# Sliding-window attention in a two-layer decoder trunk: probabilities times values with the values as stationary operand, in split single-pass form

## What is computed

```python
def swa_sink_attention(q, k, v, sinks):
    # 16 query heads on 2 key/value heads of 64; blocks of 128 queries; keys: 16 meta, previous block, own block
    k_all, v_all = band(k), band(v)
    s = jnp.einsum('bnqkgd,bnskd->bnkgqs', qb, k_all) * (DH_B ** -0.5)
    s = jnp.where(allowed[None, :, None, None], s, NEG_INF)
    mx = jnp.maximum(jnp.max(s, axis=-1, keepdims=True), sink)
    pr = jnp.exp(s - mx)
    denom = jnp.sum(pr, axis=-1, keepdims=True) + jnp.exp(sink - mx)
    w = pr / denom
    o = jnp.einsum('bnkgqs,bnskd->bnqkgd', w, v_all)

# a layer, as a whole
mixed = concat([ya * silu(ga), yb * silu(gb), yc * silu(gc)])   # HGRN2 recurrence, attention, pooling
return h + mixed @ w_out
```

## Time and profile before

| what | value |
|---|---|
| median of three runs | 1631.59 us |
| the profiled execution's own time | 1631.37 us |
| its span in the profile | 1629.6 us |
| PE / PEld busy | 99% / 91% |
| DVE / ACT / POOL busy | 56% / 40% / 1% |
| TensorE clock granted | full (2.4 GHz) |
| share of PE in the chain that ended last | 96% |

### The profile page before, as it was taken

The page is one execution under the profiler, slowest core; times in us unless marked ns, Lnnn a source line. Parts: engine busy times, 40 slices in busy tenths (PEclk is TensorE's granted clock), DMA queues, the critical chain, the costliest instruction groups (busy, mean ns, idle before and its releaser), DMA issues.

```text
span 1629.6 us, 27470 instructions
## 1 busy us (share of the span) xinstructions
PE 1609.7 (99%) x11174; PEld 1481.2 (91%) x11174; DVE 915.1 (56%) x1897; ACT 645.5 (40%) x1280; POOL 20.8 (1%) x78
## 2 busy tenths in 40 slices
PE   6999999999999999999999999999999999999999
PEld 6999999999999999999998899888999878888887
DVE  7777877645666554434335678774555664443231
ACT  7676455423223332323237774553223233232121
POOL 0000000000000000000000000000000000000000
PEclk9999999999999999999999999999999999999999
DMA  6222211112121222434342221111212212234441
GB/s 252 84 100 78 79 34 46 53 53 78 53 78 53 80 102 85 150 118 157 118 144 79 103 78 53 53 52 53 78 53 78 72 59 101 81 130 138 135 156 65
DMA packets 28013, 147.22 MB, mean 90 GB/s; under 512 B 3568, under 2 KB 3696, under 8 KB 12656
## 3 DMA queue, kind: packets, MB, share of 16 engines
q1 hardware_dynamic: 27888, 145.46, 25.5%
HBM read 136.86 MB, written 8.52 MB: 89 GB/s over the span
## 4 chain that ended last, share of the span: by engine, by line
PE 96%; DVE 2%; issue 1%; ACT 0%; DMA 0%; SPq 0%; DVEq 0%
PE ps_gemm L798 80%; PE ps_mix L688 3%; PE ps_mix L724 3%; PE ps_mix L640 2%; PE ps_mix L654 2%; PE ps_mix L683 1%; PE ps_gemm L616 1%; DVE rstd L883 1%; PE ps_mix L768 1%; PE ps_mix L770 0%; PE ps_mix L700 0%; PE ps_mix L757 0%; PE ps_mix L719 0%; DVE w_lo L865 0%; DMA w_stage<-in_w_in 0%
## 5 line engine op out<-in xcount | busy, mean ns | idle before, releaser
L798 PE MATMUL ps_gemm<-x_hi,w_hi 128*128 128x264 f32 (+1 forms) x2240 | 560.7, 315 | 12.4 <-DVE w_lo L865 10.2
L798 PE MATMUL ps_gemm<-x_hi,w_lo 128*128 128x264 f32 (+1 forms) x2240 | 542.3, 307 | 0.0
L798 PE MATMUL ps_gemm<-x_lo,w_hi 128*128 128x264 f32 (+1 forms) x2240 | 541.8, 307 | 0.0
L798 PEld LDWEIGHTS ps_gemm<-x_hi,w_hi 128*128 128x128 f32 x2240 | 363.5, 189 | 34.9 <-DVE w_lo L865 11.0
L798 PEld LDWEIGHTS ps_gemm<-x_hi,w_lo 128*128 128x128 f32 x2240 | 363.1, 189 | 19.3
L798 PEld LDWEIGHTS ps_gemm<-x_lo,w_hi 128*128 128x128 f32 x2240 | 362.5, 189 | 16.4
L865 DVE TENSOR_TENSOR w_lo<-w_stage,w_hi 128x512 fp32r<-128x512 f32 x464 | 305.5, 689 | 104.0 <-ACT w_hi L422 92.6
L422 ACT ACTIVATE w_hi<-w_stage 128x512 fp32r<-128x512 f32 x464 | 265.4, 618 | 169.5 <-DVE z L943 122.7
L798 PE MATMUL ps_gemm<-mixed_hi,w_lo 128*128 128x264 f32 (+1 forms) x768 | 205.3, 322 | 0.0
L798 PE MATMUL ps_gemm<-mixed_lo,w_hi 128*128 128x264 f32 (+1 forms) x768 | 205.0, 321 | 0.0
L798 PE MATMUL ps_gemm<-mixed_hi,w_hi 128*128 128x264 f32 (+1 forms) x768 | 203.8, 320 | 0.0
(11 more groups left out here) (169 smaller groups left out, 1407.4 us busy)
## 6 DMA issues: line engine op xcount, KB each, us to landing
w_stage<-in_w_in SPq DMA_DIRECT2D x83, 1024.0 KB, 4.8
w_stage<-in_w_out SPq DMA_DIRECT2D x32, 1024.0 KB, 5.2
x_in<-in_xT SPq DMA_DIRECT2D x4, 1056.0 KB, 9.9
res<-in_xT SPq DMA_DIRECT2D x16, 264.0 KB, 5.4
h1T<-z SPq DMA_DIRECT2D x16, 264.0 KB, 5.8
res<-h1T SPq DMA_DIRECT2D x16, 264.0 KB, 5.2
out<-z SPq DMA_DIRECT2D x16, 256.0 KB, 5.5
rope<-in_c_rope SPq DMA_DIRECT2D x2, 528.0 KB, 4.7
```

The lines of the kernel that those rows point to most:

```text
L798: ins = pe.matmul(g[:, bank, 0:size], ws, xs[:, k, c:c + size], start=tick == 0 and i == 0, stop=tick == TICKS - 1 and i == 2)
```

## The change

- **Values as weights.** `values` now makes the output with head dimensions as rows and the queries of two heads as 256 moving columns. The values `a_v` are split in high and low halves side by side in the 128 weight columns; the transposed probabilities are split too (`a_pt_hi` by ScalarE, `a_pt_lo` by VectorE, `att_probs_low`). All are float32r. Rows of the other 64 hold the product with the low half of the values; ScalarE copies them out (`a_out_lo`), VectorE adds (`att_out`), for each batch, straight into `y`. `outputs_t` and `att_normalise` go.
- **Meta keys.** GpSimd splits the meta columns in two instructions; VectorE spreads the transposed ones into a block-diagonal operand of 512 columns (L1171 of the new kernel), and one float32r matmul of 128 rows takes them with `a_vmeta`. Its values are loaded by eight small transfers instead of four.
- **Reciprocals at the end.** The sums of all batches are collected in `a_den`; after the last batch VectorE inverts them, TensorE transposes them, SyncE writes them to memory and loads them spread over 64 rows (slots 22 and 24; 16 transfers for each half in layer 0, 8 in layer 1); VectorE multiplies four tiles of `y` in slot 23 and four in slot 25, tick 6.
- **The table.** Jobs are now spaced by the batch: 1.0 tick for b = 0, 1.6 for b = 1, 1.9 for the others.
- **Order on VectorE.** In a tick the low halves and the sums stand ahead of the meta spread and the masked maximum.
- **GpSimd takes `w_lo`** for the chunks 12 to 20 of a layer, which is made in slots 11 to 19.
- In slot 2 ScalarE copies the values in four pieces and VectorE takes four differences.

```diff
-    if at < 0 or (at and at * 5 // 8 == (at - 1) * 5 // 8):
+CELL_TICKS = {0: 1.0, 1: 1.6, 2: 1.9, 3: 1.9, 4: 1.9}
+LEAD_TICKS, TAIL_TICKS, TAIL_CELLS = 1.0, 1.2, 18
+RECIP_LOAD_SLOTS, RECIP_SLOTS, RECIP_TICK = (22, 24), (23, 25), 6
+WLO_POOL = range(ATT_SLOT + 1, 21)
...
# SyncE
+                if n == RECIP_LOAD_SLOTS[0]:
+                    rows = 4 * len(ATT_B[layer])
+                    sp.wait_ge(s_rde, layer + 1)
+                    sp.dma_start(rdD[0:rows], rdt[0:rows]).then_inc(s_rdo, 16)
+                    sp.wait_ge(s_rdo, 16 * (layer + 1))
+                    load_recips(layer, 1)
+                if n == RECIP_LOAD_SLOTS[1]:
+                    sp.wait_ge(s_rdm, 8 * layer + 4)
+                    load_recips(layer, 0)
...
# GpSimd
+            def w_low(N, q):
+                pool.wait_ge(s_whi, 4 * N + q + 1)
+                pool.tensor_tensor(wl[:, N % 3, ks], wst[:, N % 3, ks], wh[:, N % 2, ks].bitcast(F32), ALU.subtract)
+            def probs_meta(layer, q, pair):
+                pool.tensor_copy(pmc[0:nq, Q % 2, 0, heads], src).then_inc(s_apc, 1)
+                pool.wait_ge(s_apc, 2 * Q + pair + 1)
+                pool.tensor_tensor(pmc[0:nq, Q % 2, 1, heads], src, pmc[0:nq, Q % 2, 0, heads].bitcast(F32),
+                                   ALU.subtract).then_inc(s_apm, 1)
...
# ScalarE, lag OUT_LAG = 13
+                        act.wait_ge(s_apv, 2 * Q + 2)
+                        act.activation(ol[rows, 0:4 * nq], M[other, 3, 0:4 * nq], ACT.Copy).then_inc(s_aol, 1)
...
# TensorE
+            def values(layer, q, pair):
+                if pair == 0 and Q:
+                    pe.wait_ge(s_aod, Q)
                 if b:
-                    for i in range(4):
-                        for s in range(0 if b >= 2 else 1, 2):
-                            last = pe.matmul(o[:, DH * i:DH * i + DH], pts[:, i // 2, i % 2, s],
-                                             vb[:, b - 1 + s, DH * kv:DH * kv + DH],
-                                             start=False, stop=i == 3 and s == 1)
+                    pe.wait_ge(s_apl, pairs_before(layer, q) + pair + 1)
+                    for s in range(first, 2):
+                        for part in (pth, ptl):
+                            ins = pe.matmul(M[:, 3, 256 * pair:256 * pair + 256], vs[:, b - 1 + s, kv],
+                                            part[:, s, heads].rearrange("p i q -> p (i q)"),
+                                            start=pair == 0 and s == first and part is pth, stop=False)
+                if pair == 1:
+                    pe.wait_ge(s_ame, Q + 1)
+                    pe.matmul(M[:, 3, 0:4 * nq], vm[:, kv], bd[:, :, 0:nq], start=b == 0, stop=True)\
+                      .then_inc(s_apv, 1 if b else 2)
-                pe.transpose(M[0:64, 1, BAND:BAND + nq], pmc[0:nq, Q % 2].rearrange("p i k -> p (i k)"), eye[0:nq, 0:nq])\
+                pe.transpose(M[:, 1, BAND:BAND + nq], both, eye[0:nq, 0:nq]).then_inc(s_amt, 1)
...
# VectorE
+            def att_probs_low(layer, q, pair):
+                dve.wait_ge(s_ape, no + 1)
+                signal(dve.tensor_tensor(ptl[:, first:2, heads],
+                                         M[:, 2].rearrange("p (s i q) -> p s i q", s=2, i=2)[:, first:2],
+                                         pth[:, first:2, heads].bitcast(F32), ALU.subtract), s_apl)
+            def att_apply_recips(layer, j):
+                dve.wait_ge(s_rdi, recip_loads(layer, 2 - j))
+                for i in range(4):
+                    m = 4 + 4 * j + i
+                    signal(dve.tensor_tensor(y[:, m, c], y[:, m, c], rdb[:, i, c], ALU.mult), s_rdm)
...
-                    if tick - 1 in HI_TICKS and N + 1 < NTOT:
+                    if tick - 1 in HI_TICKS and N + 1 < NTOT and not low_on_pool(N + 1):
                         w_low(N + 1, HI_TICKS.index(tick - 1))
```

More of the change, by code:

```diff
@@ L92, with recip_loads, att_cells, att_job @@
 ATT_Q0 = [0, len(ATT_B[0])]
+RECIP_LOAD_SLOTS, RECIP_SLOTS, RECIP_TICK = (22, 24), (23, 25), 6
+def recip_loads(layer, rounds):
+    return 16 * (16 * rounds if layer == 0 else 32 + 8 * rounds)
+def att_cells(layer):
+    jobs, t, at = ATT_B[layer], 0.0, {}
+    for c in range(ATT_LEAD + 4 * len(jobs) + TAIL_CELLS):
+        at[int(t)] = c
+        q = (c - ATT_LEAD) // 4
+        t += LEAD_TICKS if q < 0 else TAIL_TICKS if q >= len(jobs) else CELL_TICKS[jobs[q][0]]
+    return at
+ATT_CELL = [att_cells(l) for l in range(DEPTH)]
+def att_job(layer, n, tick):
+    at = (n - ATT_SLOT) * TICKS + tick - ATT_TICK
+    return ATT_CELL[layer][at] if at in ATT_CELL[layer] else None
+WLO_POOL = range(ATT_SLOT + 1, 21)
+def low_on_pool(N):
+    return N % NC in WLO_POOL
+def lows_before(N, pool):
+    return 4 * sum(low_on_pool(M) == pool for M in range(N))
 def pairs_before(layer, q):
@@ L297, in att_at @@
         def att_at(layer, n, tick, lag):
-            job = att_job(n, tick)
+            job = att_job(layer, n, tick)
             if job is None:
@@ L315, in att_pair_at @@
         def att_pair_at(layer, n, tick, job):
-            now = att_job(n, tick)
+            now = att_job(layer, n, tick)
             if now is None:
@@ L334, in load_w, with load_recips @@
                 sp.dma_start(wst[:, N % 3].rearrange("p k c -> p (k c)"), src).then_inc(s_w[N % 3], 16)
+            def load_recips(layer, j):
+                blocks = len(ATT_B[layer]) // 4
+                all_ = rdD[0:16 * blocks].rearrange("(b j v i) q -> j v i b q", j=2, v=2, i=4)
+                for kv in range(2):
+                    rows = slice(64 * kv, 64 * kv + 64)
+                    for i in range(4):
+                        real = all_[j, kv, i, blocks - NBLK:].unsqueeze(0).broadcast_to([64, NBLK, P])
+                        sp.dma_start(rdb[rows, i, N_META:].rearrange("p (b q) -> p b q", b=NBLK), real)\
+                          .then_inc(s_rdi, 16)
+                        if blocks > NBLK:
+                            meta = all_[j, kv, i, 0, 0:N_META].unsqueeze(0).broadcast_to([64, N_META])
+                            sp.dma_start(rdb[rows, i, 0:N_META], meta).then_inc(s_rdi, 16)
             def load_x(q):
@@ L820, in _ @@
                     at = att_at(layer, n, tick, VALUE_LAG)
-                    if at and at[1] == 0:
-                        values(layer, at[0])
+                    if at and at[1] < 2:
+                        values(layer, *at)
                     at = att_at(layer, n, tick, PAIR_LAG)
@@ L825, in _ @@
                         probs_t(layer, at[0], at[1] // 2)
[L826 to L828 removed]
+                    at = att_at(layer, n, tick, RECIP_T_LAG)
+                    if at and at == (len(ATT_B[layer]) - 1, 0):
+                        recips_t(layer)
                     h, r = hgrn_at(n, tick)
@@ L1249, in _ @@
                                                      ALU.subtract), s_ql)
+                    at = att_at(layer, n, tick, PAIR_LAG + 1)
+                    if at and at[1] % 2 == 1 and ATT_B[layer][at[0]][0]:
+                        att_probs_low(layer, at[0], at[1] // 2)
+                    at = att_at(layer, n, tick, OUT_LAG + 1)
+                    if at and at[1] == 0:
+                        att_out(layer, at[0])
                     at = att_at(layer, n, tick, META_LAG)
```

234 lines of the change are left out of this document (131 added, 103 removed).

## The result

The changed kernel takes **1642.88 us** (median of 4 runs, 1640.65 to 1646.06) against 1631.59 (1631.11 to 1631.74): ratio 1.0071, 95% interval 1.0056 to 1.0086. It is 0.7% slower; I had forecast 1602.4, and the result lies above the range. The profiled execution took 1643.33 us, its span is 1641.5.

The account below looks back on a forecast made before the run. TensorE's own work was taken to bound the kernel as long as VectorE keeps up. From 1631.4 us, -42.4 (TensorE), +9.4 (VectorE late in attention) and +4.0 (reciprocals) gave 1602.4 us, range 1589 to 1622.

Parts of the forecast that it names:

- TensorE, -42.4: TensorE's own work: cheaper values and meta keys, no transposes back, small additions; -42.4 us, between -45.4 and -39.6.
- rival 4: Value matmuls: the halves bring nothing if 256 columns take 0.31 us; +42 us, 1635 us in all; chance 0.04.
- The reciprocals, +4.0: Slot 25, tick 6: four VectorE multiplications delay TensorE's next level by 2.0 us in each layer, +4.0 us; slot 23 costs 0.
- GpSimd's hold, 1.5 us a slot: Attention slots: GpSimd subtractions keep VectorE's instructions with two SBUF inputs waiting, 1.5 us a slot (0 to 4).
- Rival 3: Slots 12 to 18 and 70 to 75: GpSimd subtractions stop VectorE for their whole 1.6 us; +81, 1674 us; chance 0.06.
- What reaches the end, +9.4: Attention: VectorE's time, with GpSimd's hold added, exceeds TensorE's in seven tight slots; +9.4 us, +0.5 without the hold.
- the seven slots to which I gave 9.4 us: Slots 12, 13, 14, 18, 71, 72 and 75, where VectorE was to exceed TensorE by 0.9 to 1.9 us each.
- The second: Attention: VectorE falls further behind, needing to be on time within a job; twice the 9.4, or late reciprocals; 1611 to 1622; 0.12.
- The first: Attention: VectorE keeps up and the hold costs nothing that reaches TensorE; 1593.5 us, or 1589; chance 0.25.

Follow-up runs that it names:

- e4: Changed kernel, nobody making the weights' low halves for chunks 12 to 20, and output copy and sum one job earlier: 1595.17 us, ratio 0.9778.
- e6: Changed kernel with output copy and sum one job earlier and the second four reciprocal multiplications in slot 26 instead of 25: 1608.4 us, ratio 0.9859.
- e1: Changed kernel with nobody making the weights' low halves for chunks 12 to 20 (third product takes the high half again): 1608.8 us, ratio 0.9862.
- e3: Changed kernel with ScalarE's output copy and VectorE's sum one job earlier (OUT_LAG 12 instead of 13): 1615.58 us, ratio 0.9904.
- e5: Changed kernel with all low halves of the weights back on VectorE and output copy and sum one job earlier: 1615.89 us, ratio 0.9908.

## Why the prediction was wrong

- **TensorE, -42.4: right, a little small.** Busy time fell by 45.4 us where little disturbs it (e4), and e4 still has one stretch of 3.4 us at half clock, so the work itself fell by up to 1.7 more. That is the outer end of my range; its own terms (0.115 a value matmul, entries and weights free) add up to -46.1, not the -45.4 I wrote. Value matmuls start 0.12 apart and the one for the meta keys takes 0.23; rival 4 fell.
- **The reciprocals, +4.0: right.** 3.8 by the lengths of slots 25 and 83 (e6), 3.8 of idle time in these slots in the change, where slot 83 has a stretch at half clock on top. The multiplications are 0.70 us each, and the 16 transfers were in time.
- **GpSimd's hold, 1.5 us a slot: right in size, in part by luck.** VectorE's busy time was lengthened by 28.8 us over 18 slots (957.5 against e1's 928.7), 1.6 a slot. The subtraction took 1.34 us instead of 1.06. Rival 3 had each one stop VectorE for 1.0 us or more; it is 0.36 to 0.40. My formula (share of the slot times half a subtraction, for 9 to 13 instructions) gives 2.2 to 2.9 us a slot with the measured 1.34 us and GpSimd's 7.2 to 7.3 us in slots 16 and 13, so it met 1.6 only because the subtraction was taken too short. I also counted instructions with two SBUF inputs only, and the four-element negation with one was lengthened as well. The trace agrees with the rule that I cited from the Trainium skill, "SBUF — State Buffer", section "Who interferes with whom", for the pairs with two SBUF inputs. The same section says that a `tensor_scalar`, which the negation is, can contend with GpSimd too, in its modes with two ports; I had left that half of the rule out, and the 169 to 353 ns of the negation fit it.
- **What reaches the end, +9.4: this is the step that failed.** I set VectorE's time in a slot against TensorE's, and let everything vanish that fitted ("a lag of about two jobs (some 4 us) less a tick's work is absorbed, not more"). That holds for neither of the two waits that it names. From the sum to the next values there is one job, as I had written in the sentence before it ("due one job ahead"), and from a low half to the next transposes there is one too; one job is some 2.4 us. Each batch passes through the loop once, and any lateness over its lead is idle time of TensorE there and then, however empty VectorE is later in the slot; while TensorE stands, VectorE waits too (the meta spread L1171 waited for scores of TensorE for 20.3 us in the change and 4.5 in e3). So the seven slots to which I gave 9.4 us idle for 18.4, and the others, to which I gave 1.7 us of room or more and no cost, idle for 15.4 (slots 15 to 17 and 19 for 0.9 to 2.0 us each): 33.8 in place of 9.4. I had named the right wait and its lead, and let twice that lead be absorbed. With a lead of two jobs (e3) the wait for the sum is gone.
- **A term was missing:** TensorE's clock. With the idle time came another 19.8 us of longer busy time, up to 15 of it at half clock. I had read full clock in every window before, but TensorE was never idle in those windows, so they could not show what idle time does. Both terms together, not the loop alone, make the change slower than the kernel before: the new idle time by itself, 37.5 us, is less than the 45.4 gained.
- **The rivals.** The second (VectorE must be on time within a job) had the mechanism, but I priced it at twice the 9.4, another sum over slots, instead of by turns of the loop: 22 waits for the sum, in 32 batches with b of 1 or more, of 1.2 us each (27.0) are most of what came. A slower kernel I had given 0.08. The first was what the same code gives once the two causes are out.

## What to carry to other kernels

Where an in-order engine feeds another at fixed lags, compare lateness with the lead of each single wait, counted in the table from the instruction that frees a buffer to the one that takes it, and not with the free time of a stage; check first whether a lag can simply be made one job longer. Elementwise work given to GpSimd relieves VectorE by less than its own duration where VectorE works in SBUF, so measure what is left of the relief. And idle time of TensorE has a second price when its clock falls after it.

## What the runs showed that I had not expected

- GpSimd's 72 subtractions cost VectorE 26 to 29 us of busy time (34.9 in the kernel before), all of it in instructions that touch only SBUF, down to one of four elements; VectorE making them itself is 44.5 us (973.4 less 928.9). The relief is 40% of what it seems, and worth nothing once the loop is loose (e3 and e5).
- Pauses of TensorE of 1.1 to 2.7 us (in slot 12 two, of 0.92 and 1.15 us, before 175.5 and 176.85) are followed by 3.4 or 6.8 us at granted clock 0.50. It did not come each time: e5 idled for 21.5 us in attention in pauses of up to 2.4 us and had no such stretch there. What decides is not shown by these runs.
